# A hybrid encoder block on one core: VectorE makes the low parts of the pair tiles, some VectorE steps are reordered, and the weight sums begin four tiles sooner

## The reference, cut to what matters

```
h  = rms(x) * g_mix;  za, zu, zv, zq, zg = split(h @ w_in)
ya = (gelu(s5(za)) * sigmoid(gelu(s5(za)) @ w_glu + b_glu)) @ w_a_out
yb = (gelu(zu) * (tril(w_s) applied to layernorm(gelu(zv)) + b_s)) @ w_b_out
yc = attention(zq over k, v = rms(mem) @ w_kv; 4 heads of 128) @ w_c_out
x  = x + (sigmoid(zg + b_gate) weighted sum of ya, yb, yc) @ w_out
hf = rms(x) * g_ffn
x  = x + (silu(hf @ w_gate) * (hf @ w_up)) @ w_down
out = rms(x) * g_final
```

## Time and profile before

| | |
|---|---|
| median of 3 runs | 773.86 us (773.61, 773.86, 775.49) |
| the profiled execution, its own time | 775.70 us |
| its span in the trace | 774.0 us |
| TensorE busy | 752.6 us, 97% |
| VectorE busy | 574.4 us, 74% |
| ScalarE busy | 389.4 us, 50% |
| GpSimd busy | 304.7 us, 39% |
| mean share of the 16 DMA engines | 71% (53.0% + 17.4% + 0.4%) |

### The profile page before, as it was taken

How to read it: one execution, slowest core, us unless ns; L and a number is a source line. 1 busy time by engine, 2 the same in 40 slices (tenths; PEclk the granted TensorE clock), 3 DMA queues, 4 the chain that set the end, 5 groups by cost and what they waited for, 6 DMA issues and landing times.

```text
span 774.0 us, 10786 instructions
## 1 busy us (share of the span) xinstructions
PE 752.6 (97%) x4066; PEld 644.9 (83%) x4066; DVE 574.4 (74%) x858; ACT 389.4 (50%) x576; POOL 304.7 (39%) x216
## 2 busy tenths in 40 slices
PE   9999998999999999999999999989999999999997
PEld 7788876688888888888888787879999999788886
DVE  6999999766666666246665779967978888636687
ACT  6896565653636343643344425345545455434554
POOL 5456575156363636456565655440000000740000
PEclk9999999999999999999999999999999999999999
DMA  8645767167666678687878898776867665867853
GB/s 288 267 159 195 238 194 217 55 185 198 184 195 185 199 206 266 196 239 222 236 207 233 236 296 236 223 196 199 239 211 225 218 197 187 300 222 262 281 206 127
DMA packets 58339, 166.77 MB, mean 215 GB/s; under 512 B 6960, under 2 KB 9136, under 8 KB 51504
## 3 DMA queue, kind: packets, MB, share of 16 engines
q1 hardware_dynamic: 53744, 139.61, 53.0%
q0 software_dynamic: 4400, 26.22, 17.4%
q10 hardware_dynamic: 144, 0.26, 0.1%
HBM read 158.99 MB, written 59.51 MB: 282 GB/s over the span
## 4 chain that ended last, share of the span: by engine, by line
PE 35%; POOL 26%; issue 24%; DVE 8%; DMA 5%; ACT 2%; SPq 0%; POOLq 0%; ACTq 0%
POOL w_lo L614 19%; PE bank L1962 7%; PE bank L1964 7%; PE bank L1963 7%; PE bank L2384 4%; PE bank L2385 4%; PE bank L2386 4%; POOL sum_dram L631 3%; DMA raw<-w_dram 3%; POOL mix_dram L631 2%; DVE tab_tmp L1207 2%; DMA raw<-sum_dram 2%; DVE w_lo L1207 1%; POOL w_lo L619 1%; POOL w_lo L705 1%
## 5 line engine op out<-in xcount | busy, mean ns | idle before, releaser
L614 POOL TENSOR_TENSOR w_lo<-raw,w_hi 128x1024 fp32r<-128x1024 f32 x62 | 152.7, 2463 | 176.8 <-ACT w_hi L715 176.8
L715 ACT ACTIVATE w_hi<-raw 128x1024 fp32r<-128x1024 f32 x84 | 89.0, 1060 | 183.6 <-PE bank L1964 150.3
L1962 PE MATMUL bank<-h_hi,w_hi 128*128 128x512 f32 (+1 forms) x480 | 164.9, 344 | 2.9 <-POOL w_lo L619 2.7
L1964 PE MATMUL bank<-h_hi,w_lo 128*128 128x512 f32 (+1 forms) x480 | 163.1, 340 | 0.0
L1963 PE MATMUL bank<-h_lo,w_hi 128*128 128x512 f32 (+1 forms) x480 | 163.0, 340 | 0.0
L1962 PEld LDWEIGHTS bank<-h_hi,w_hi 128*128 128x128 f32 x480 | 91.1, 190 | 14.0 <-issue 3.5
L1964 PEld LDWEIGHTS bank<-h_hi,w_lo 128*128 128x128 f32 x480 | 91.0, 190 | 10.2
L1963 PEld LDWEIGHTS bank<-h_lo,w_hi 128*128 128x128 f32 x480 | 91.1, 190 | 9.8 <-issue 0.2
L619 POOL TENSOR_TENSOR w_lo<-raw,w_hi 128x512 fp32r<-128x512 f32 x48 | 68.8, 1468 | 52.5 <-ACT w_hi L715 47.4
L1962 PE MATMUL bank<-hu_hi,w_hi 128*128 128x512 f32 x128 | 51.2, 400 | 6.0 <-POOL w_lo L614 5.3
L1029 ACT ACTIVATE w_hi<-raw 128x1024 fp32r<-128x1024 f32 x32 | 33.8, 1057 | 37.4 <-PE bank L1964 23.6
(11 more groups left out here) (366 smaller groups left out, 1890.4 us busy)
## 6 DMA issues: line engine op xcount, KB each, us to landing
raw<-w_dram SPq DMA_DIRECT2D x68, 512.0 KB, 4.1
sum_dram<-ff_dram SPq DMA_DIRECT2D x28, 512.0 KB, 6.2
mix_dram<-down_dram SPq DMA_DIRECT2D x22, 512.0 KB, 6.5
raw<-sum_dram SPq DMA_DIRECT2D x37, 256.0 KB, 3.3
raw<-ff_dram SPq DMA_DIRECT2D x16, 512.0 KB, 4.2
sum_dram<-ff_dram POOLq DMA_DIRECT2D x14, 512.0 KB, 7.1
sum_dram<-sum_dram POOLq DMA_DIRECT2D x28, 256.0 KB, 5.6
raw<-ff_dram SPq DMA_DIRECT2D x27, 256.0 KB, 2.9
```

Of the source, the lines that this page charges most:

```text
L614: nc.gpsimd.tensor_tensor(w_lo[:, s, :], raw[:, s, :], fv(w_hi[:, s, :]), ALU.subtract).then_inc(w_ready, 1)
L715: nc.scalar.activation(w_hi[:, slot, :], raw[:, slot, :], ACT.Copy).then_inc(w_rounded, 1)
L1962: mm(out, a[0], b[0], start=first, stop=False)
L1964: return mm(out, a[1], b[0], start=False, stop=last)
```

## The change

It has three parts.
- In the attention part, VectorE makes `vM` ahead of the second half of the last table products, and `head_scale(3)` and `scale_u(3)` ahead of `table_sum(0)` and `table_sum(1)` respectively.
- A new constant `T_DVE = T_FF + 4`: from this tile on the low parts are made by VectorE (`low_plain`), 12 tiles, each placed behind a step that waits for TensorE's tile t - 2 or near it. They count on `w_ready_dve`, so all waits on those counts move (`tile_low`, `low_done`, `unit_split`). GpSimd keeps only the sums' DMAs there. ScalarE's order in the pairs changes too: each `split_hidden` moves ahead of a rounding, and rounding 14 ahead of the copies of h's forms.
- `T_MIX` is 4 less: copies and adds of the weight sums come four tiles earlier.

```diff
-T_MIX = T_QK + 4
+T_MIX = T_QK
+T_DVE = T_FF + 4
-L_DN = T_ST
+L_DN = T_DVE
...
         def low_done(eng, n):
-            eng.wait_ge(w_ready_dve, n + 1)
+            eng.wait_ge(w_ready_dve, T_ST - T_DVE + n + 1)
+        def tile_low(eng, t):
+            if t < T_DVE:
+                eng.wait_ge(w_ready, t + 1)
+            else:
+                eng.wait_ge(w_ready_dve, t - T_DVE + 1)
...
             def next_weights(t):
-                sp.wait_ge(w_ready, t + 1 - RAW)
+                tile_low(sp, t - RAW)
...
-            for t in range(T_J1 + NS, T_ST):
+            for t in range(T_J1 + NS, T_DVE):
                 low_weights(t % NS, t)
                 weight_sums(t - NS)
+            for t in range(T_DVE, T_ST):
+                tile_low(pool, t)
+                weight_sums(t - NS)
...
 (ScalarE)
             round_weights(T_FF + 4)
             feed_forward(0)
-            for j in (5, 6):
-                round_weights(T_FF + j)
+            round_weights(T_FF + 5)
             split_hidden(0)
+            round_weights(T_FF + 6)
+            round_normed(range(0, 4))
             round_weights(T_FF + 7)
             feed_forward(1)
-            round_normed(range(0, 4))
+            round_normed(range(4, 8))
             round_weights(T_FF + 8)
-            round_normed(range(4, 8))
...
             split_hidden(2)
-            act.wait_ge(normed, 18)
+            round_weights(T_FF + 14)
+            act.wait_ge(normed, 20)
             nc.scalar.activation(t2_hi[:, :, :], xT[:, 4:8, HALF:T], ACT.Copy).then_inc(normed_hi, 1)
...
             nc.scalar.activation(t4_hi[:, :, :], xT[:, 4:8, 0:HALF], ACT.Copy).then_inc(normed_hi, 1)
-            round_weights(T_FF + 14)
...
 (VectorE)
             head_max(3)
-            table_half(NC // 2, (1,))
             dve.wait_ge(w_used, T_VU + 7)
             for c in range(2):
                 V.tensor_scalar(vM[:, c, :], bank[4 + c][:, :], mtrstd[:, c:c + 1], None, ALU.mult
                                 ).then_inc(v_taken, 1)
+            table_half(NC // 2, (1,))
+            head_scale(3)
             go(table_sum(NC // 2, 0))
+            scale_u(3)
             table_sum(NC // 2, 1).then_inc(tables_ready, 1)
-            head_scale(3)
-            scale_u(3)
...
+            def low_plain(t):
+                dve.wait_ge(w_rounded, t - 1)
+                tt(w_lo[:, t % NS, :], raw[:, t % NS, :], fv(w_hi[:, t % NS, :]), ALU.subtract).then_inc(w_ready_dve, 1)
...
-            for n in range(2):
-                scaled_up(0, n)
+            scaled_up(0, 0)
+            low_plain(T_FF + 4)
+            scaled_up(0, 1)
+            low_plain(T_FF + 5)
             hidden_sums(0)
             low_hidden(0)
             scaled_gate(1, 0)
+            low_plain(T_FF + 6)
             norm_rows(range(0, 4))
             scaled_gate(1, 1)
+            low_plain(T_FF + 7)
             norm_rows(range(4, 8))
             scaled_up(1, 0)
+            low_plain(T_FF + 8)
             low_rows(range(0, 4))
             scaled_up(1, 1)
+            low_plain(T_FF + 9)
             hidden_sums(1)
             low_hidden(1)
...
             scaled_gate(3, 0)
+            low_plain(T_FF + 14)
             low_forms_a()
             scaled_gate(3, 1)
+            low_plain(T_FF + 15)
             low_forms_b()
```

More of the change, by code:

```diff
@@ L529, in load_forms @@
                 elif n < 3:
-                    sp.wait_ge(w_ready, T_ST - 2 + n)
+                    tile_low(sp, T_ST - 3 + n)
                 else:
@@ L1052, in _ @@
             feed_forward(0)
-            for j in (5, 6):
-                round_weights(T_FF + j)
+            round_weights(T_FF + 5)
             split_hidden(0)
+            round_weights(T_FF + 6)
+            round_normed(range(0, 4))
             round_weights(T_FF + 7)
             feed_forward(1)
-            round_normed(range(0, 4))
+            round_normed(range(4, 8))
             round_weights(T_FF + 8)
-            round_normed(range(4, 8))
-            for j in (9, 10):
-                round_weights(T_FF + j)
+            round_weights(T_FF + 9)
             split_hidden(1)
+            round_weights(T_FF + 10)
             round_weights(T_FF + 11)
             feed_forward(2)
-            for j in (12, 13):
-                round_weights(T_FF + j)
+            round_weights(T_FF + 12)
+            round_weights(T_FF + 13)
             split_hidden(2)
-            act.wait_ge(normed, 18)
+            round_weights(T_FF + 14)
+            act.wait_ge(normed, 20)
             nc.scalar.activation(t2_hi[:, :, :], xT[:, 4:8, HALF:T], ACT.Copy).then_inc(normed_hi, 1)
-            act.wait_ge(normed, 20)
+            nc.scalar.activation(h_hi[:, 0:4, HALF:T], xT[:, 0:4, 0:HALF], ACT.Copy).then_inc(normed_hi, 1)
             nc.scalar.activation(t4_hi[:, :, :], xT[:, 4:8, 0:HALF], ACT.Copy).then_inc(normed_hi, 1)
-            round_weights(T_FF + 14)
-            nc.scalar.activation(h_hi[:, 0:4, HALF:T], xT[:, 0:4, 0:HALF], ACT.Copy).then_inc(normed_hi, 1)
+            round_weights(T_FF + 15)
             act.wait_ge(normed, 22)
             nc.scalar.activation(xT_r[:, 0:4, 0:HALF], xT[:, 0:4, HALF:T], ACT.Copy).then_inc(normed_hi, 1)
-            round_weights(T_FF + 15)
             feed_forward(3)
@@ L1714, in _, with forms_of_h_a @@
             x21, x22 = xT[:, 4:8, 0:HALF], xT[:, 4:8, HALF:T]
-            def forms_of_h():
+            def forms_of_h_a():
                 dve.wait_ge(normed, 16)
@@ L1721, in forms_of_h, with forms_of_h_b @@
                 tt(x12, x12, x22, ALU.subtract)
+            def forms_of_h_b():
                 tt(x22, x22, x11, ALU.add).then_inc(normed, 1)
@@ L1735, in low_forms_b @@
             def low_forms_b():
+                dve.wait_ge(normed_hi, KD + 3)
                 tt(xT_r[:, 4:8, 0:HALF], x21, fv(t4_hi[:, :, :]), ALU.subtract)
@@ L1769, in _ @@
             scaled_gate(2, 0)
+            low_plain(T_FF + 10)
             low_rows(range(4, 8))
             scaled_gate(2, 1)
-            forms_of_h()
+            low_plain(T_FF + 11)
+            forms_of_h_a()
             scaled_up(2, 0)
+            low_plain(T_FF + 12)
+            forms_of_h_b()
             scaled_up(2, 1)
+            low_plain(T_FF + 13)
             hidden_sums(2)
@@ L1980, in tile_ready @@
             def tile_ready(t):
-                pe.wait_ge(w_ready, t + 1)
+                tile_low(pe, t)
             def h(k):
@@ L2412, in _ @@
                 else:
-                    tile_ready(L_DN)
+                    pe.wait_ge(w_ready, L_DN + 1)
                 pe.wait_ge(ff_lo, k + 2)
```

10 lines of the change are left out of this document (5 added, 5 removed).

## The result

| | before | after |
|---|---|---|
| median, runs of the same chip | 773.74 us (771.02 to 775.49, 4 runs) | 761.16 us (759.45 to 761.67, 4 runs) |
| the profiled execution, its own time | 775.70 | 761.58 |
| its span | 774.0 | 759.8 |

The ratio is 0.9837, 95% interval 0.9804 to 0.9870: 12.6 us or 1.6% faster. The forecast was 765.8 with a range of 763.6 to 769.5.

A forecast was written before the change was run, and what follows sets the result against it. TensorE, busy 752.6 of 774.0 us, bounds the kernel; only idle time and lowered clock can be won. -3.04 - 1.93 - 3.69 - 1.67 + 0.5 = -9.8 us from 775.7 gives 765.9, forecast 765.8, range 763.6 to 769.5.

The forecast's parts named there:

- Part 1: End of the attention part: `vM` and the reciprocal ahead of table steps gain 3.04 us, bounds 1.4 to 3.04.
- The 1.37 at `vM` and the 1.67 at `prob`: TensorE's waits in the attention part, before `values(0)` and for head 3's scalings; both would go.
- The cover of 1 us: TensorE's other work hides the late `table_sum(1)` by 1 us; if that fails, up to 1 us returns.
- The gaps at tiles 8 and 14: Plain feed-forward pairs: TensorE's idle gaps of 1.93 and 3.69 us, waiting for GpSimd low parts, would go.
- the low clock: Behind tile 14's gap, ten matmuls at 1.2 GHz take 3.95 us instead of 2.28; the 1.67 would go.
- Tile 6: Plain pairs: load issued 1.4 us later, landing 453.3 to 455.9, low part needed 457.1; loss 0 to 1.2, taken 0.5.
- Part 3: Weight sums four tiles earlier, first copies near 41 to 63 us: taken at 0, bounds +1.5 and -0.7.
- the likeliest case: The summed gains alone, spanning 764.7 (tile 6 free, all won) to 767 us.
- (a): Rival, chance 0.17: full DMA queues in 440 to 456 us make tile 6 and a neighbour 1 to 2 late; 767.5 to 768.
- (b): Rival, chance 0.12: in-order VectorE reaches tile 8 or 14 late by 1.5 to 3 us; 767.5 to 769.5.
- (c): Rival, chance 0.05: feed-forward part yields nothing, another chain (loads) being just behind; 772.7 us.
- (d): Rival, chance 0.05: traffic makes VectorE's passes long, low parts cost 2.5 us there too; slower, 785 us.

The follow-up runs named there:

- a_act: Kernel before with only ScalarE's new order in the plain pairs, GpSimd still making all low parts; 766.22 us, ratio 0.9908.
- b_pool: Changed kernel, but GpSimd makes all low parts of the pair tiles; 762.69 us, ratio 0.9879 to the kernel before.
- after_again: Changed kernel, unedited, measured once more; 762.49 us, ratio 0.9872 to the kernel before.
- b_mix1: Changed kernel with the weight sums only one tile earlier than before (`T_MIX = T_QK + 3`); 760.66 us, ratio 0.9836 to the kernel before.
- c_x1: Changed kernel with SP's stores of x1 four tiles later, behind the loads of tiles 8 and 9; 759.88 us, ratio 0.9834 to the kernel before.
- c_x1_nomix: Changed kernel with the stores of x1 four tiles later and the weight sums at their old tiles; 763.94 us, ratio 0.9885 to the kernel before.
- before_again: Kernel before, unedited, profiled once more; 773.21 us, ratio 1.0013.
- a_vm: Kernel before with only `vM` and `head_scale(3)` moved ahead of the table steps; 770.47 us, ratio 0.9968.
- a_mix: Kernel before with only the weight sums four tiles earlier; 771.68 us, ratio 0.9974.
- a_dve: Kernel before with only VectorE's low parts and ScalarE's new order in the pairs, sums and attention order as before; 764.77 us, ratio 0.9891.

## Why the prediction was right or wrong

**Part 1, right.** The 1.37 at `vM` and the 1.67 at `prob` went, and nothing came back at the table sums. By ratio the part alone gives 2.5 us (0.9 to 4.1) for the 3.04 forecast, and a_act's profile, unchanged up to there, shows that the 1.67 isn't there in every execution. My picture of the passes was off in one place: I had said that the products would start behind GpSimd's pass and take 2.4 us together. They met it again, and the second took 3.41. The cover of 1 us held. The reading of `vM` in the rows was wrong: it ran while GpSimd stood idle (131.40 to 132.81, between the passes that end at 130.29 and start at 133.53), so its 0.7 us say nothing for "one with a single SBUF input isn't held", and the 128x2 `TENSOR_SCALAR` at 88.25, which has a single one, took 3.17 instead of 0.17.

**Part 2, the gaps right, the cause mixed.** The gaps at tiles 8 and 14 and the low clock went, 1.93 + 3.69 + 1.67. The last term was taken from one profile; in the other three it is 1.7, 2.6 and 2.9. I priced the engine and the order as one and had written of tile 14 that "the diff puts it ahead of both"; the runs show that the order alone suffices (a_act) and that the engine adds nothing measurable to it (b_pool beside after_again). Part 2 alone gives 8.4 us (6.7 to 10.0), with no wait at tile 6, for 7.29 forecast without that term.

**Tile 6, mis-sized.** Taken at 0.5 of 0 to 1.2; it measured 1.47, and 1.17 in the second profile. The mechanism was the one named. The load was issued 12.7 us ahead of TensorE's need before (457.1 - 444.40) and 11.3 after (450.48 - 439.22): 1.4 later, as worked out. The landing took 10.2 us, just past the far end of the 7.5 to 10.1 that my 453.3 to 455.9 meant; the 0.5 that I took meant about 9.4. In b_mix1 the wait is 2.46, with a low clock behind it, so the bound of 1.2 was too small.

**Part 3 taken at 0: the number held in the changed kernel, by luck.** Bounds +1.5 and -0.7. b_nomix, the changed kernel without the shift, takes 760.98 us beside 761.16 and 762.49 with it. That is no sign of a shift without effect: it removes the wait of 1.2 at `zu(3)` and makes the one at tile 6, and the two about cancel. Alone it gives 2.0 us (0.2 to 3.8). With the stores out of the way its worth shows: c_x1 is 4.1 us below c_x1_nomix, though part of that is c_x1_nomix's new wait at tile 10. I looked only at DMA room in the early stretch and at landing times. The path that mattered was another, as far as the profiles show it: the DMAs move the low parts, and the low parts decide which VectorE instruction stands still. The waits at 113 and 125 us I had set aside as ones "which the diff doesn't touch".

**The start of the sum, wrong.** This is the step that failed most clearly: "I take the two lower ones as runs without the low clock, in which only about 8.2 are to be won". The low clock behind tile 14 is in all four profiles of the old ScalarE order with GpSimd's low parts (before, before_again, a_vm, a_mix). Of 79 further executions of the kernel before, 62 have a mean granted clock of 0.997 or less, where a_act and a_dve, which lack the gap at tile 14, have 0.998 to 1.000; and the other 17 are hardly faster (median 772.9 against 773.1). So a lower time was no sign of a run without the low clock, and the median is 772.7 to 773.7 where the profiled execution took 775.70. The 9.8 us should have gone off the median: 773.7 - 9.8 = 763.9. That is 2.0 of the 4.6 us by which the forecast was too high.

The other 2.7 us are not shown to be any one thing. As a difference the sum said 9.8; the first measurement gave 12.6 (10.1 to 15.2) and after_again, by its ratio, 9.9 (7.7 to 12.0). b_nomix, which has parts 1 and 2 and no wait at tile 6, gave 11.4 (9.1 to 13.8) where the same terms make 10.3. So the terms were low by 2.8, 0.1 or 1.1 us, and only the first interval leaves the sum out. The low clock, taken at its smallest price, is a term that the profiles show too small. The low end of the range, 763.6, is part 3's 0.7 below the 764.7 of the likeliest case and 0.4 more for the spread of runs, though three runs of the kernel before already lay 1.9 us apart.

**Rivals.** (a), late landing at tile 6, happened in kind at 1.5 us, but not in time; c_x1 shows that the stores ahead of the load made it. The Trainium skill ("DMA: Bandwidth & Descriptors", "Issuing engines are not separate DMA queues") has the transfers of all issuing engines on the same 16 DMA engines. No run here shows what that costs: the stores and the load share even the issuing queue. (b) and (c) did not happen. (d), VectorE too slow, did not: the low parts cost 1.22, and VectorE's load fell.

**Left open.** Which instruction of VectorE meets which of GpSimd in each phase beyond those shown, what makes the waits of about 1 us near 30, 429 and 578 to 601 us come and go, what holds the low clock for about 3 us in some executions and 7 in others, and the 2.7 us of the forecast's miss beyond its start.

## What to carry to other kernels

A low part (or any hand-over) is late by what stands ahead of it on each engine in turn: before you move it to a faster engine, move it up in the list of the slower one, since that alone may free the gap. Subtract gains from the median, not from the profiled execution, and let a second profile tell which waits belong to the kernel and how their price varies. A shift of transfers is not without effect just because there is room in the queues: look at which waits and which meetings of VectorE with GpSimd it moves, and try the phases one by one.
